# A ring of ten slots, a selection in place, values stored by head, and pauses in the pace of a streaming encoder layer

## The reference, cut to what matters

```python
z = h @ w_in                                    # split into gq gk gv gr glr dq dk dv gates
s1 = einsum(q1, k1) * scale; s2 = einsum(q2, k2) * scale      # chunk mask for the prompt
p = softmax(s1) - lam * softmax(s2)
o_b = einsum('bhqk,bkhv->bqhv', p, v)           # v: 8 heads x 128 values per token
mix = (sigmoid(g_a) * y_a + sigmoid(g_b) * y_b) @ w_out
x = x + gt1 * mix
# PEER, per token and head
v1, i1 = top_k(s1, 16); v2, i2 = top_k(s2, 16)
sc, ci = top_k(v1[:, None] + v2[None, :], 16)   # 256 candidates
idx = e1 * 128 + e2; g = softmax(sc)
act = gelu(x . peer_u[idx])
y = sum(g * act * peer_v[idx])
```

## Time and profile before

| what | value |
|---|---|
| median of 3 runs | 4812.23 us (4809.24 to 4817.81) |
| profiled execution | 4809.88 us, span 4808.1 us |
| busy share PE, DVE, ACT, POOL | 65%, 56%, 27%, 26% |
| moved | 1466.27 MB, mean 305 GB/s |
| queue of the gathers / of SyncE | 58.9% / 20.7% of the 16 DMA engines' span |

### The profile page before, as it was taken

One profiled execution on the slowest core, in us unless ns is written; L12 is line 12 of the kernel. 1 busy time (PEld: TensorE's weight loads), 2 busy tenths in 40 slices (PEclk: granted clock), 3 DMA queues, 4 the chain that ended last, 5 costly groups with the idle time before them and its releaser, 6 DMA issues.

```text
span 4808.1 us, 46328 instructions
## 1 busy us (share of the span) xinstructions
PE 3137.2 (65%) x14944; PEld 1915.3 (40%) x14944; DVE 2689.4 (56%) x7493; ACT 1308.3 (27%) x2814; POOL 1246.6 (26%) x1067
## 2 busy tenths in 40 slices
PE   6887846886797268865974397885559843333333
PEld 4675734553465035633743164552237520000000
DVE  2133145678535766786345755576542466675675
ACT  2344102455301034565010225544330200000000
POOL 0000002323223232333222322222121224444453
PEclk8886978887898578987987597787779865555555
DMA  7322439997899799988998887776577969999998
GB/s 265 131 77 90 170 103 366 365 359 298 339 362 409 281 395 361 372 314 325 366 365 328 315 322 260 275 275 250 195 265 286 350 244 371 411 408 389 395 407 338
DMA packets 284681, 1466.27 MB, mean 305 GB/s; under 512 B 46344, under 2 KB 103528, under 8 KB 118392
## 3 DMA queue, kind: packets, MB, share of 16 engines
q0 software_dynamic: 152064, 1107.36, 58.9%
q1 hardware_dynamic: 132376, 355.94, 20.7%
HBM read 1426.39 MB, written 35.68 MB: 304 GB/s over the span
## 4 chain that ended last, share of the span: by engine, by line
PE 43%; DMA 29%; DVE 13%; issue 6%; ACT 6%; SPq 2%; POOL 0%; DVEq 0%; ACTq 0%; POOLq 0%
DMA rt_ring<-in_peer_uv,rt_few_idx 15%; PE pair L567 10%; PE pair L556 9%; PE rt_acc L807 7%; PE bank L567 5%; PE bank L556 4%; DVE rt_ring L1580 4%; DMA w<-out_v_prompt 3%; PE pair L722 2%; PE bank L736 2%; DMA w<-in_weights 2%; DMA out_v_prompt<-dense 2%; DMA w<-out_v_sample 2%; DMA scratch_scores<-dense 2%; DVE rt_diag L1591 1%
## 5 line engine op out<-in xcount | busy, mean ns | idle before, releaser
L1633 POOL DMA_INDIRECT rt_ring<-in_peer_uv,rt_few_idx x1056 | 1243.3, 1177 | 3533.0 <-PE rt_acc L807 2602.7
L1580 DVE SCALAR_TENSOR_TENSOR rt_ring<-rt_ring,rt_h 128x1024 f32<-128x1024 f32 x1056 | 1264.2, 1220 | 456.6 <-DMA rt_ring<-in_peer_uv,rt_few_idx 435.8
L807 PE MATMUL rt_acc<-rt_ring,rt_diag 128*32 128x512 f32 x4224 | 811.9, 846 | 999.7 <-DVE rt_diag L1591 999.3
L807 PEld LDWEIGHTS rt_acc<-rt_ring,rt_diag 128*32 128x32 f32 x4224 | 102.0, 126 | 1445.1 <-DVE rt_diag L1591 1291.9
L567 PE MATMUL pair<-dense,w 128*128 128x256 f32 (+1 forms) x2336 | 552.7, 395 | 18.3 <-DMA w<-in_weights 17.4
L556 PE MATMUL pair<-w,dense 128*128 128x256 f32 (+1 forms) x2288 | 545.0, 396 | 17.5 <-DMA w<-in_weights 12.8
L1142 ACT ACTIVATE rt_act_dot<-rt_dot 128x2 f32<-128x2 f32 x528 | 106.3, 202 | 1578.4 <-DVE rt_ring L1580 1576.8
L567 PEld LDWEIGHTS pair<-dense,w 128*128 128x128 f32 x2336 | 446.4, 194 | 143.2 <-issue 48.2
L556 PEld LDWEIGHTS pair<-w,dense 128*128 128x128 f32 (+1 forms) x2288 | 427.5, 190 | 159.3 <-issue 63.6
L1591 DVE TENSOR_SCALAR rt_diag<-cst,rt_act_dot,rt_few_prob 128x32 f32<-128x32 f32 x1056 | 265.9, 297 | 185.8 <-ACT rt_act_dot L1142 169.5
L722 PE MATMUL pair<-w,dense 64*128 64x512 f32 (+3 forms) x448 | 137.8, 741 | 254.2 <-DMA w<-out_v_prompt 117.8
(11 more groups left out here) (236 smaller groups left out, 3066.8 us busy)
## 6 DMA issues: line engine op xcount, KB each, us to landing
w<-in_weights SPq DMA_DIRECT2D x232, 1024.0 KB, 7.1
rt_ring<-in_peer_uv,rt_few_idx POOLq DMA_INDIRECT x1056, 10.9
rt_h<-scratch_h SPq DMA_DIRECT2D x132, 128.0 KB
dense<-scratch_mod SPq DMA_DIRECT2D x18, 512.0 KB, 11.2
dense<-in_x_prompt SPq DMA_DIRECT2D x16, 512.0 KB, 9.3
scratch_scores<-dense SPq DMA_DIRECT2D x64, 128.0 KB, 7.2
rt_sc<-scratch_scores SPq DMA_DIRECT2D x8, 1024.0 KB, 9.4
rt_x<-scratch_x SPq DMA_DIRECT2D x132, 32.0 KB
```

Source lines behind the costliest of these rows:

```text
L807: mm = nc.tensor.matmul(acc[u % 2][a * T:(a + 1) * T, :], diag[b % 2][:, i, :], slot[:, D + c * BANK:D + (c + 1) * BANK], start=(q == 0), ...
L1580: dt = nc.vector.scalar_tensor_tensor(up, up, 1.0, h2[u % 2][:], ALU.mult, ALU.mult, accum_out=dot[:, b % 2, i:i + 1])
L1633: nc.gpsimd.indirect_dma_start(ring[n % RING][:], None, d["peer_uv"], bass.IndirectOffsetOnAxis(ap=few_idx[u % 2][:, c:c + 1], axis=0)).th ...
```

## The change

- RING goes from 9 to 10. The memory comes from `rt_sc2`: the selection now replaces in `rt_sc` itself.
- `dv` stores each tile's values a second time, by head, to the scratch tensor `vh` (8, 128, 1152), in pieces of 512 bytes. The attention loads its values from there, each partition in one run of up to 4 KB. The cached values are laid out by head ahead of the launch (`cache_vh`).
- The semaphores of the `vst` buffers count two transfers for each tile.
- The paced list has items `pause` that have a cost and do nothing: 8 behind the last merge step and 16 between `scores` and the first `select` piece, whose `scores` step costs nothing now. As the costs are shared out over the same number of batches, the other steps stand a little closer.
- Where a pause is in a batch, it counts in the half at which TensorE's `weigh` stands.

```diff
-B, RING = 2, 9
+B, RING = 2, 10
@@ ticks
-    out.append((("merge", g, 32), 0.5))
+    out += [(("merge", g, 32), 0.5), (("pause",), 8.0)]
@@ sequence
-        lane = ticks(g + 1) + [(i, 1.5) for i in select(GROUPS[g + 1][0])] if g + 1 < NG else []
+        lane = []
+        if g + 1 < NG:
+            first = select(GROUPS[g + 1][0])
+            lane = ticks(g + 1) + [(first[0], 0.0), (("pause",), 16.0)] + [(i, 1.5) for i in first[1:]]
@@ dv on ScalarE, and the like where all stores are waited for
-                    act.wait_ge(v_out[v % 3], 16 * (v // 3))
+                    act.wait_ge(v_out[v % 3], 32 * (v // 3))
@@ top16
-                        m = nc.vector.match_replace(spare[:, j, :], top[:, j, 0:8], values[:, j, :], FAR)
+                        m = nc.vector.match_replace(values[:, j, :], top[:, j, 0:8], values[:, j, :], FAR)
@@ load_weights
-                    sp.dma_start(dst[:, D:D + nk].rearrange("p (t c) -> p t c", c=VD),
-                                 d["v_prompt"][0, 0, 0:nk, h, :].rearrange("(t p) c -> p t c", p=P)).then_inc(at_, 16)
+                    sp.dma_start(dst[:, D:D + nk], d["vh"][h, :, 0:nk]).then_inc(at_, 16)
...
-                    sp.dma_start(dst[:, D:D + PAST].rearrange("p (t c) -> p t c", c=VD),
-                                 d["cache_v"][0, 0, :, h, :].rearrange("(t p) c -> p t c", p=P)).then_inc(at_, 16)
-                    sp.dma_start(dst[0:DEC, D + PAST:D + PAST + VD], d["v_sample"][0, 0, :, h, :]).then_inc(at_, 16)
+                    sp.dma_start(dst[:, D:D + PAST], d["cache_vh"][h]).then_inc(at_, 16)
+                    sp.dma_start(dst[0:DEC, D + PAST:D + PAST + VD], d["vh"][h, 0:DEC, NT * VD:(NT + 1) * VD]).then_inc(at_, 16)
@@ dv on SyncE
                     sp.dma_start(dst[:, 2 * i:2 * i + 2, :].rearrange("t h v -> t (h v)"), vst[0:n, v % 3, :]).then_inc(v_out[v % 3], 16)
+                    sp.dma_start(d["vh"][2 * i:2 * i + 2, 0:n, t * VD:(t + 1) * VD].rearrange("h p c -> p h c"),
+                                 vst[0:n, v % 3, :].rearrange("p (h c) -> p h c", h=2)).then_inc(v_out[v % 3], 16)
```

More of the change, by code:

```diff
@@ L399, in trunk @@
         gate2 = sb("rt_gate2", [P, 2, QC])
-        sc, sc2 = sb("rt_sc", [P, 2 * PH, NKEY]), sb("rt_sc2", [P, 2 * PH, NKEY])
+        sc = sb("rt_sc", [P, 2 * PH, NKEY])
         val, ind, indf = sb("rt_val", [P, 2 * PH, TOPK]), sb("rt_ind", [P, 2 * PH, TOPK], U32), sb("rt_indf", [P, 2 * PH, TOPK])
         cand = sc[:].rearrange("p (h e) n -> p h (e n)", e=2)
-        cand2 = sc2[:].rearrange("p (h e) n -> p h (e n)", e=2)
         pick = sc[:].rearrange("p j (k i) -> p (j k) i", i=TOPK)
@@ L962, in place_qk @@
                             act.wait_ge(kr_out[i], 16 * max(rows_stored(r) for r in range(g * 8 + 4) if r % 3 == i))
-                            act.wait_ge(v_out[i], 16 * ((4 * FIRST[g] + 4 * len(GROUPS[g]) + 2 - i) // 3))
+                            act.wait_ge(v_out[i], 32 * ((4 * FIRST[g] + 4 * len(GROUPS[g]) + 2 - i) // 3))
                         for i in range(2):
@@ L1506, in select, with top16 @@
                 maps, heads = range(2 * PH), range(PH)
-                def top16(rows, values, spare, top, where):
+                def top16(rows, values, top, where):
                     for j in rows:
@@ L1520, in top16 @@
                     for j in rows:
-                        m = nc.vector.max(top[:, j, 8:16], spare[:, j, :])
+                        m = nc.vector.max(top[:, j, 8:16], values[:, j, :])
                         if j % 4 == 3:
@@ L1525, in top16 @@
                     for j in rows:
-                        m = nc.vector.max_index(where[:, j, 8:16], top[:, j, 8:16], spare[:, j, :])
+                        m = nc.vector.max_index(where[:, j, 8:16], top[:, j, 8:16], values[:, j, :])
                         if j % 4 == 3:
@@ L1529, in top16 @@
                     settle(m)
-                yield from top16(maps, sc, sc2, val, ind)
+                yield from top16(maps, sc, val, ind)
                 pair = val[:].rearrange("p (h e) k -> p h e k", e=2)
@@ L1538, in select @@
                 yield
-                yield from top16(heads, cand, cand2, best, pos)
+                yield from top16(heads, cand, best, pos)
                 nc.vector.tensor_tensor(below[:], best[:], best[:, :, 0:1].to_broadcast([P, PH, TOPK]), ALU.subtract).then_inc(shifted, 1)
@@ L1664, in stored @@
                 for i in range(3):
-                    sp.wait_ge(v_out[i], 16 * ((nv + 2 - i) // 3))
+                    sp.wait_ge(v_out[i], 32 * ((nv + 2 - i) // 3))
                 for i in range(2):
@@ L1879, in _ @@
                 sp.sem_clear(s)
-SCRATCH = {"mod": (2, 4 * D), "kT": (DH, P, TOK), "x1": (TOK, D), "h2": (TOK, D), "scores": (TOK, 2 * PH, NKEY)}
+SCRATCH = {"mod": (2, 4 * D), "kT": (DH, P, TOK), "vh": (DH, P, (NT + 1) * VD), "x1": (TOK, D), "h2": (TOK, D), "scores": (TOK, 2 * PH, NKEY)}
 def _unit(i, name):
@@ L1901, in _inputs @@
     i = {k: np.ascontiguousarray(v) for k, v in inputs.items()}
-    out = {k: i[k] for k in ("x_prompt", "x_sample", "c_prompt", "c_sample", "cache_v", "state_gla", "norm1_gain", "norm2_gain",
+    out = {k: i[k] for k in ("x_prompt", "x_sample", "c_prompt", "c_sample", "state_gla", "norm1_gain", "norm2_gain",
                              "b_mod", "w_alpha")}
@@ L1905, in _inputs @@
     out["cache_kT"] = np.ascontiguousarray(i["cache_k"][0, 0].transpose(1, 2, 0))
+    out["cache_vh"] = np.ascontiguousarray(i["cache_v"][0, 0].reshape(PAST // P, P, DH, VD).transpose(2, 1, 0, 3)).reshape(DH, P, PAST)
     out["weights"] = np.stack([_unit(i, name) for name in HOST])
```

## The result

The changed kernel takes 4767.62 us, the median of 5 runs (4755.80 to 4779.30), beside 4812.23 us for the kernel before (5 runs, 4798.81 to 4817.81). The ratio is 0.9914, with an interval of 0.9890 to 0.9938: 0.9% faster, 41 us by the ratio. The forecast was 4700, that is 112 us less. The direction was right, the size was not: under half of it came.

A forecast was written before the change was run, and what follows sets the result against it. Stages A and B were taken as nearly transfer-bound, C as set by the lane, the last by gathers. -69 - 48 - 27 + 32 = -112 from 4809.9 gives 4698, taken as 4700 us; range 4600 to 4825.

The forecast's parts named there:

- What bounds the kernel: Whole kernel: stages A and B nearly bound by transfers, C by the lane, the last by gathers; fill without gathers.
- Values in one run: Attention's loads of values in A, B and C: one run per partition lands sooner, shortening TensorE's waits; -69 us.
- The tenth slot: Gather ring: second gather issued one batch earlier, fewer VectorE waits; -22 in A, -22 in B, -4 in C, -48 us.
- Pauses: Lane's mix and selection: waits for gates and scores shrink; 5 in A, 7 in B, 15 in C, sum -27 us.
- The second store: Values' store in `dv`: small pieces delay ScalarE; 10 each in A, B and C, 2 in the fill, +32 us.
- In place, 0: Selection replacing in its own buffer: same instructions on the same shapes, one buffer less; 0 us.
- The half of `weigh`: TensorE's `weigh` stands behind the lane steps in six batches with a pause; 0 us, ends -3 and +6.
- Rival 2: Ring and pauses bring nothing, as the lane's own chain fills every batch; -37, 4775 us, chance 0.17.
- Rival 1: Store pieces bound the `dv` steps, +114, making the kernel slower; 4843 us, chance 0.12.
- Rival 3: Engines couple more strongly than counted: ring -110, pauses -60, stores cost 20; -219, 4593 us, chance 0.12.
- rival 5: TensorE's waits for values only become VectorE and ScalarE waits, ring and stores cancel; 4802 to 4822 us, chance 0.07.
- Rival 4: DMA queue turns carry many pieces: loads -10, stores +11, rest unchanged; -74, 4738 us, chance 0.07.

The follow-up runs named there:

- the fast version: Four weight buffers instead of three and values stored by head and loaded in one run, nine slots, no pauses, against the kernel before: 4618.08 us, 0.9600.

## Why the prediction was wrong, step by step

**What bounds the kernel.** The five stages, and which of them could move, were right: fill and last stage stood still. That C is set by the lane was right as well, and more so than I used it.

**Values in one run, -69: the step that failed, together with the next.** Measured 35 (give or take 12). "For six waits in C I take 3 us less each", and 4 each for the seven of the sample: together 46 us for C, and it was 5.8 of waits (17.5 with the second store on both sides). The premise that failed is that "a piece of SyncE's queue costs a gather's piece of 8 KB (...) whatever its own size is". The earlier trace rows are from a stretch of stores and weights with the gathers' queue always full; in the waits of C 765 pieces passed beside 127. Two more things are wrong in the term. The 7.1 us of a weight came from the whole run; the three weights that land in the stretch of C's attention take longer:

```profile
w<-in_weights SPq DMA_DIRECT2D x3, 1024.0 KB, 8.2
```

And, the larger, I asked how long a load takes with the gathers always beside it, where a load that is asked for at the last moment stops the gathers itself, and then lands with them. The prediction priced this at 0 for the sample's half of the waits and then took a value six tenths of the way to the other end. Its sign for this, landings near 7 us in place of 9.7, has no number in the profile of the changed kernel; from issue to use the loads took as long as before (10.3 and 10.4 us). With the second store on both sides the waits for values fell by 45 us in all, 10 in A, 17 in B and 17.5 in C, for the 35 of time.

**The tenth slot, -48: failed.** Measured 12.5. The count of waits was right nearly to the microsecond (47 less in the kernel with the ring alone), the exchange rate was not. I let a wait for a gather that goes away be time that is won, though the prediction itself says that the gain is there only where the DMA engines would have stood idle: the DMA share in A and B, 0.90 and 0.90, became 0.91 and 0.90 in that kernel. Both steps of the ring, eight to nine and nine to ten, gave a quarter of the waits as time. Where the other three quarters go isn't shown: in the kernel with ten slots the waits for values sum to 190.2 us (192.2 before) and those at the mix to 48.1 (43.7), which is far from the 35 us that are missing.

**Pauses, -27: the sum nearly right, its terms not.** Measured 19. In place they bring 33, the pace costs 14, for which the prediction had 0; it named this end ("if the steps that move closer wait for as much"). "The waits for `scratch_scores` at the lane's end gone or below 5 us" was wrong: behind three batches 48 us of them are left. VectorE waits longer in front of its last copies instead, for the key scores' own stores, 59.1 against 41.7 us in the whole run. Why three batches were not enough isn't shown; the batches in between bring gathers of their own to the same DMA engines.

**The second store, +32: too high.** Measured 15 (7 to 24), near the lower end of 11 that the bytes alone give. ScalarE's waits for the stores of values grew in that kernel by 25 us, from 91.9 to 116.6, more than the time did.

**In place, 0** was never timed alone; the instruction takes 275 ns with one buffer as with two, and the fourth buffer that it paid for is where the value of this edit lies. **The half of `weigh`** was not run alone.

**The sum.** By parts: loads +34, store -17, ring +35, pauses +8 against the forecast; 61 us together, and the remaining 10 are within the intervals.

**The rivals.** Rival 2's 4775 is the nearest number, for a wrong reason: ring and pauses together bring 29 us, and the loads half of its 69. Rival 1 fell, as the store costs 15 and not 114. Rival 3 fell, and rival 5 too (4802 to 4822). Rival 4 had 10 for the loads, against 35 (give or take 12) here and 35 net of the store with a fourth buffer. It was built on the Trainium skill, "DMA: Bandwidth & Descriptors", Queues, rings and completion order, which has an engine drain several descriptors of one ring before it turns, by which 512-byte pieces would travel together. While both queues were full the counts disagree (528 and 528 packets in ten us, 3.82 and 0.32 MB). Where the gathers ran out the pieces went many to one (765 beside 127), but whether by that rule or because some engines had no gathers left, no view here tells.

**What stays open.** Where three quarters of the ring's saved waits went. Why the faster pace costs 63 us on the fast version and 14 on the one before; a different meeting of steps and batches is what its attention stretch shows, but no run sets that meeting by itself. And the dial of free batches goes in one direction on the kernel before, while on the other six and ten can't be told apart and three and fourteen are slower.

## What to carry to other kernels

Before you make a late load faster, ask why it is late: if its buffer came free just before it was needed, the load's own speed hardly counts, and one more buffer there can be worth ten times what the same memory is worth elsewhere (158 us against 12.5). Then the shape of the load can come to matter, so look at it again once the buffer is there. And price what a pause or a slot does to the rest of the order by a run of its own that has the same cost in a place where it can help nothing: it tells the gain in place from the price of the pace.

## What the runs showed of the hardware

- A wait for a load of 512-byte pieces and one for the same bytes in runs of 4 KB ended equally late (14.2 and 14.5 us, 864 and 480 packets) when 4.1 MB of gathers went beside them and no new one could be issued. With 2.3 MB it was 9.8 us.
- Four loads of 1.05 MB, each beside 2.10 MB of gathers, took 10.2 to 11.3 us from issue to use with the values in 1024 pieces of 512 bytes, and 10.3 to 11.3 with the values in one run for each partition.
- With the gathers' queue at 92% of the engines the two queues moved packet for packet: 528 and 528 in ten us, 3.82 and 0.32 MB. In one of the waits, once its last gather was out, it was 127 and 765 in four us. With the fourth buffer, loads in 512-byte pieces left 50.0 us of waits in one stage and loads in one run 6.6.
- Of VectorE's waits for gathers about a quarter was time, in both directions of the ring's size (47 us of waits for 12.5, 74 for 19).
- The replacement in place takes as long as into a second buffer, 275 ns for 128 values in each partition.
- Executions of one kernel on one chip spread by 10 to 20 us to either side (12 runs of the kernel with the pauses: 4774.14 to 4807.41, median 4796.45), so that a profiled execution by itself can show a third of a gain (ring and pauses: 11 us of 29) or twice the gain (six free batches: 57 of 27). Stage by stage comparisons of single profiles are to be read with that in mind.
